# Values and three query units from rows that are not yet normed, and three exponentials some units later

## What is computed

```python
def rmsnorm(x, g):
    return x * rsqrt(mean(x * x, axis=-1) + EPS) * g

h = rmsnorm(x, g_mix)
q, k, v, f_logit, gb, gc_in, xc, g_attn, g_conv = split(h @ w_in)
attn = forgetting_attention(q, k, v, f_logit + b_f)          # 8 heads of 64
conv = gb * causal_depthwise_conv(gc_in * xc, conv_w)
x = x + (gated sum of the two branches) @ w_out
h = rmsnorm(x, g_ffn)
q = h @ w_q                                                  # 8 heads x 2 halves of 128
s1, s2 = q_half1 @ k1.T, q_half2 @ k2.T                      # scores against 128 keys each
v1, i1 = top_k(s1, 16); v2, i2 = top_k(s2, 16)
top_s, top_j = top_k(v1[:, None] + v2[None, :], 16)          # best 16 of 256 pairs
gates = softmax(top_s)
x = x + sum over the chosen 16384-expert ids of gates * gelu(h @ u[id]) * v[id]
...                                                          # a gated embedding and a last norm follow
```

## Time and profile before

| | |
|---|---|
| median of 3 runs | 1810.73 us (1810.68 to 1811.7) |
| the profiled execution, its own time | 1813.05 us |
| its span in the trace | 1810.3 us |
| TensorE busy | 1774.5 us, 98% of the span |
| VectorE, GpSimd, ScalarE busy | 1082.2, 916.2, 671.6 us |
| mean granted clock of TensorE | 0.996 of full speed |

### The profile page before, as it was taken

One profiled execution on the slowest core, in us unless ns is written; L12 is line 12 of the kernel. 1 busy time (PEld: TensorE's weight loads), 2 busy tenths in 40 slices (PEclk: granted clock), 3 DMA queues, 4 the chain that ended last, 5 costly groups with the idle time before them and its releaser, 6 DMA issues.

```text
span 1810.3 us, 22222 instructions
## 1 busy us (share of the span) xinstructions
PE 1774.5 (98%) x7972; PEld 1454.8 (80%) x7972; DVE 1082.2 (60%) x1929; ACT 671.6 (37%) x1031; POOL 916.2 (51%) x742
## 2 busy tenths in 40 slices
PE   6999999989999999999999999999999999999998
PEld 5777788878878788888888888888888888888886
DVE  6355521436799988862222221235888888888874
ACT  5434332333332222322222222244444444444464
POOL 6323244334336787776666666405566666664200
PEclk9999999989999999999999999999999999999999
DMA  5212122317775444444444444467999999999821
GB/s 193 88 59 71 59 93 93 116 59 312 269 242 176 148 144 145 147 146 146 146 146 144 148 146 134 144 214 249 371 374 367 373 361 382 381 364 379 318 82 47
DMA packets 155565, 360.99 MB, mean 199 GB/s; under 512 B 32064, under 2 KB 73024, under 8 KB 155328
## 3 DMA queue, kind: packets, MB, share of 16 engines
q1 hardware_dynamic: 100976, 257.47, 41.4%
q0 software_dynamic: 34816, 67.41, 10.4%
q10 hardware_dynamic: 19664, 34.70, 5.3%
HBM read 298.44 MB, written 61.01 MB: 199 GB/s over the span
## 4 chain that ended last, share of the span: by engine, by line
PE 92%; DVE 6%; ACT 1%; DMA 1%; issue 1%; ACTq 0%; DVEq 0%
PE pair L748 33%; PE pair L556 18%; PE pair L558 18%; PE pair L557 18%; PE pair L652 1%; PE pair L672 1%; PE pair L726 1%; DVE topj L1383 1%; DVE wl L1357 1%; DVE top L1381 1%; PE pair L642 0%; DVE earlier L1454 0%; DVE cand L1452 0%; DVE cand L1449 0%; PE pair L757 0%
## 5 line engine op out<-in xcount | busy, mean ns | idle before, releaser
L510 POOL DMA_INDIRECT gates<-gate_val,gate_at x384 | 415.1, 1081 | 203.8 <-issue 102.5
L1357 DVE TENSOR_TENSOR wl<-raw,wh 128x1024 fp32r<-128x1024 f32 x254 | 309.5, 1220 | 345.2 <-ACT wh L896 344.8
L896 ACT ACTIVATE wh<-raw 128x1024 fp32r<-128x1024 f32 x339 | 356.7, 1054 | 135.9 <-PE pair L558 123.2
L748 PE MATMUL pair<-hh,wh 128*128 128x512 f32 x1024 | 399.0, 390 | 3.6 <-ACT gout L1069 2.9
L748 PE MATMUL pair<-hl,wh 128*128 128x512 f32 x1024 | 398.6, 389 | 0.0
L748 PE MATMUL pair<-hh,wl 128*128 128x512 f32 x1024 | 398.5, 389 | 0.0
L493 POOL TENSOR_TENSOR wl<-raw,wh 128x1024 fp32r<-128x1024 f32 x85 | 207.2, 2443 | 332.7 <-ACT wh L896 332.7
L556 PE MATMUL pair<-wh,act_h 128*128 128x512 f32 x768 | 299.1, 389 | 0.0
L558 PE MATMUL pair<-wh,act_l 128*128 128x512 f32 x768 | 298.9, 389 | 0.0
L557 PE MATMUL pair<-wl,act_h 128*128 128x512 f32 x768 | 298.9, 389 | 0.0
L1069 ACT ACTIVATE gout<-pair 128x512 f32<-128x512 f32 x128 | 76.4, 597 | 471.9 <-PE pair L748 471.9
(11 more groups left out here) (234 smaller groups left out, 1907.1 us busy)
## 6 DMA issues: line engine op xcount, KB each, us to landing
raw<-stream SPq DMA_DIRECT2D x338, 512.0 KB, 3.6
score_dram<-gout ACTq DMA_DIRECT2D x128, 256.0 KB, 2.0
gates<-zeros SPq DMA_DIRECT2D x48, 512.0 KB, 6.0
score_in<-score_dram SPq DMA_DIRECT2D x128, 192.0 KB, 6.4
gate<-gates SPq DMA_DIRECT2D x128, 192.0 KB, 6.8
gates<-gate_val,gate_at POOLq DMA_INDIRECT x384
x<-xT SPq DMA_DIRECT2D x4, 512.0 KB, 5.2
picked<-score_dram,score_at POOLq DMA_INDIRECT x128, 5.7
```

The lines of the kernel that those rows point to most:

```text
L510: nc.gpsimd.indirect_dma_start(gate_list, bass.IndirectOffsetOnAxis(ap=gate_at[:, r, k:k + 1], axis=0), gate_val[:, r, k:k + 1], None).the ...
L748: last = nc.tensor.matmul(psum[u % 2][:], w(weights, U_DENSE + u, c), halves[:, c, :], start=c == 0 and which == 0, stop=c == DC - 1 and w ...
L896: nc.scalar.activation(wh[:, n % SL, :], raw[:, n % RAW, :], ACT.Copy).then_inc(hi_done, 1)
L1357: nc.vector.tensor_tensor(wl[:, n % SL, :], raw[:, n % RAW, :], wh[:, n % SL, :].bitcast(F32), ALU.subtract).then_inc(low_own, 1)
```

## The change

Values. The high and low parts of the V stage are taken from gain * x instead of the normed h (`plain_high`, `plain_low`), and the four copies out of PSUM carry `factor` as their scale. So V no longer waits for the norm. Each unit's 24 matmuls now go in three groups of eight (high, low activations, low weights); the norm's sums stand behind the first group of the second unit, and its rows behind that unit. The normed `hh` and `hl` are written into the same buffers afterwards, each pair of chunks once its V unit is done; the f logits read them. SyncE loads x and weight units in turns: x0, unit 0, x1, unit 1, x2, x3, unit 2.

Queries. The first three query units read `xh` and `xl`, made from gain * x chunk by chunk during the output units; `factor` is the scale of four copies of each unit's scores. The sums stand inside the first query unit, the rows behind it. Units 0 and 1 are no longer interleaved. The normed chunks are made beside these three units and are needed by the fourth.

Both norms keep their squares and products in PSUM (banks 4 and 5) instead of SBUF, and the table of Sqrt is loaded ahead. The exponentials of the second to fourth routing tile stand three dense units later; the first stays.

```diff
+PLAIN_PQ = 3
...
-EXP_AT = (3, 16, 32, 48)
+EXP_AT = (3, 19, 35, 51)
...
-        sq1 = gout[:, 0:2, :]
-        hf1 = gout[:, 2:4, :]
...
+        xh = sb("xh", [P, DC, T], F32R, plain)
+        xl = sb("xl", [P, DC, T], F32R, plain)
...
+                for i in {0: (0,), 1: (1,), 2: (2, 3)}.get(n, ()):
+                    load_x(i)
...
+            def values(j, part, weights, first, last_part):
+
+                for c in (2 * j, 2 * j + 1):
+                    if part is hl:
+                        pe.wait_ge(xl_ready, c + 1)
+                    elif first:
+                        pe.wait_ge(xh_ready, c + 1)
+                    for tt in range(TT):
+                        last = nc.tensor.matmul(psum[tt][:], part[:, c, tt * P:(tt + 1) * P],
+                                                weights[:, U_V + j, (c % 2) * CW:(c % 2 + 1) * CW],
+                                                start=first and c == 0, stop=last_part and c == DC - 1)
+                return last
...
-            norm_sums(0)
+            for j in range(4):
+                pe.wait_ge(hi_done, U_V + j + 1)
+                values(j, hh, wh, True, False)
+                if j == 1:
+                    norm_sums(0)
+                values(j, hl, wh, False, False)
+                wait_low(pe, U_V + j)
+                values(j, hh, wl, False, True).then_inc(unit_used, 1)
+                if j == 1:
+                    norm_rows(0)
             pe.wait_ge(wf_split, 1)
-            for j in range(4):
-                wait_low(pe, U_V + j)
-                for c in (2 * j, 2 * j + 1):
-                    pe.wait_ge(h_ready, c + 1)
-                    for tt in range(TT):
-                        cols = slice(tt * P, (tt + 1) * P)
-                        wc = slice((c % 2) * CW, (c % 2 + 1) * CW)
-                        last = three(psum[tt][:], hh[:, c, cols], hl[:, c, cols], wh[:, U_V + j, wc], wl[:, U_V + j, wc],
...
-                last = three(psum[4][0:HEADS, :], wf_h[:, c, :], wf_l[:, c, :], hh[:, c, :], hl[:, c, :], c == 0, c == DC - 1)
+                pe.wait_ge(h_ready, c + 1)
+                last = three(psum[6][0:HEADS, :], wf_h[:, c, :], wf_l[:, c, :], hh[:, c, :], hl[:, c, :], c == 0, c == DC - 1)
...
-            norm_sums(1)
...
-            pe.wait_ge(wo_out, DC)
-            project_pair(U_PQ, 0, h_ready, DC)
-            score(0)
-            for n in range(2, N_PQ):
-                pe.wait_ge(pq_out, n - 1)
-                project(U_PQ + n, n % 2)
-                score(n - 1)
+            pe.wait_ge(wo_out, DC - 2)
+            for n in range(N_PQ):
+                if n < PLAIN_PQ:
+                    if n >= 2:
+                        pe.wait_ge(pq_out, n - 1)
+                    wait_low(pe, U_PQ + n)
+                    plain_query(n, 0, 5)
+                    if n == 0:
+                        norm_sums(1)
+                    plain_query(n, 5, DC)
+                    if n == 0:
+                        norm_rows(1)
+                else:
+                    pe.wait_ge(pq_out, n - 1)
+                    if n == PLAIN_PQ:
+                        pe.wait_ge(h_ready, 2 * DC)
+                    project(U_PQ + n, n % 2)
+                if n >= 1:
+                    score(n - 1)
...
-            def square(k, sqb, c):
+            def square(k, c):
                 if c >= 2:
                     act.wait_ge(sq_used, DC * k + c - 1)
-                nc.scalar.activation(sqb[:, c % 2, :], x[:, c, :], ACT.Square).then_inc(sq_ready, 1)
+                nc.scalar.activation(psum[4 + c % 2], x[:, c, :], ACT.Square).then_inc(sq_ready, 1)
...
+            def normed_high(k, c):
+
+                act.wait_ge(hf_ready, DC * k + c + 1)
+                nc.scalar.activation(hh[:, c, :], psum[4 + c % 2], ACT.Copy).then_inc(hh_ready, 1)
+
+            def plain_high(k, high_part, c):
+
+                nc.scalar.activation(high_part[:, c, :], x[:, c, :], ACT.Copy, scale=gain[:, k, c:c + 1]).then_inc(xh_ready, 1)
...
+            act.wait_ge(consts, 6)
+            nc.scalar.activation(spare[:, 0:1], eps[:], ACT.Sqrt)
+            act.wait_ge(gain_in, 16)
+            for i in range(2):
+                act.wait_ge(x_in[i], 16)
+                plain_high(0, hh, 2 * i)
+                plain_high(0, hh, 2 * i + 1)
+                if i == 0:
+                    high(0)
+                square(0, 2 * i)
+                square(0, 2 * i + 1)
+            high(1)
+            for i in range(2, 4):
+                act.wait_ge(x_in[i], 16)
+                square(0, 2 * i)
+                square(0, 2 * i + 1)
+            for c in range(4, DC):
+                plain_high(0, hh, c)
+            high(2)
+            root(0)
+            high(3)
             for c in range(DC):
-                act.wait_ge(x_in[c // 2], 16)
-                square(0, sq, c)
-            high(0)
-            norm(0, hf, highs=((0, 1), (2, 2), (4, 3), (6, 4)))
-            for n in range(5, SL):
-                high(n)
+                if c == 6:
+                    act.wait_ge(unit_used, U_V + 4)
+                    for tt in range(TT):
+                        last = nc.scalar.activation(v_sb[:, tt, :], psum[tt][:], ACT.Copy, scale=factor[:, tt:tt + 1])
+                    last.then_inc(v_out, 1)
+                elif c % 2 == 0:
+                    act.wait_ge(unit_used, U_V + c // 2 + 1)
+                normed_high(0, c)
+                if c < 4:
+                    high(4 + c)
             for n in range(3):
                 next_high(U_V + n)
...
                 act.wait_ge(wo_out, c + 1)
-                square(1, sq1, c)
+                square(1, c)
+                plain_high(1, xh, c)
                 if c < DC - 1:
                     next_high(U_OUT + c)
-            norm(1, hf1)
-            next_high(U_OUT + DC - 1)
-
+            root(1)
...
+                if n < PLAIN_PQ:
+                    for tt in range(TT):
+                        last = nc.scalar.activation(scores[:, n % 2, tt, :], psum[2 + n % 2][:, tt * NK:(tt + 1) * NK], ACT.Copy,
+                                                    scale=factor[:, tt:tt + 1])
+                    last.then_inc(sc_out, 1)
+                    return
...
+            query_out(0)
+            for c in range(DC):
+                normed_high(1, c)
+                if c == 3:
+                    query_out(1)
+                elif c == 5:
+                    next_high(U_OUT + DC - 1)
+            next_high(U_PQ)
+            score_out(0)
+            next_high(U_PQ + 1)
+            for n in range(2, N_PQ):
+                query_out(n)
                 next_high(U_PQ + n)
-                if n >= 1:
-                    score_out(n - 1)
+                score_out(n - 1)
...
-            def add_square(k, sqb, c):
+            def add_square(k, c):
                 dve.wait_ge(sq_ready, DC * k + c + 1)
                 if c == 0:
-                    nc.vector.tensor_copy(rstd[:], sqb[:, 0, :]).then_inc(sq_used, 1)
+                    nc.vector.tensor_copy(rstd[:], psum[4]).then_inc(sq_used, 1)
                 else:
                     dve.wait_ge(sq_used, DC * k + c)
-                    nc.vector.tensor_tensor(rstd[:], rstd[:], sqb[:, c % 2, :], ALU.add).then_inc(sq_used, 1)
-
-            def norm(k, hfb):
+                    nc.vector.tensor_tensor(rstd[:], psum[4 + c % 2], rstd[:], ALU.add).then_inc(sq_used, 1)
...
-                        nc.vector.scalar_tensor_tensor(out=hfb[:, c % 2, :], in0=x[:, c, :], scalar=gain[:, k, c:c + 1],
+                        nc.vector.scalar_tensor_tensor(out=psum[4 + c % 2], in0=x[:, c, :], scalar=gain[:, k, c:c + 1],
...
-                        nc.vector.tensor_tensor(hl[:, c - 1, :], hfb[:, (c - 1) % 2, :], hh[:, c - 1, :].bitcast(F32),
+                        nc.vector.tensor_tensor(hl[:, c - 1, :], psum[4 + (c - 1) % 2], hh[:, c - 1, :].bitcast(F32),
...
+            def plain_low(k, high_part, low_part, c):
+
+                dve.wait_ge(xh_ready, DC * k + c + 1)
+                nc.vector.scalar_tensor_tensor(out=low_part[:, c, :], in0=x[:, c, :], scalar=gain[:, k, c:c + 1],
+                                               in1=high_part[:, c, :].bitcast(F32), op0=ALU.mult,
+                                               op1=ALU.subtract).then_inc(xl_ready, 1)
+
+            for i in range(2):
+                plain_low(0, hh, hl, 2 * i)
+                plain_low(0, hh, hl, 2 * i + 1)
+                add_square(0, 2 * i)
+                add_square(0, 2 * i + 1)
+            for c in range(4, DC):
+                add_square(0, c)
+            for c in range(4, DC):
+                plain_low(0, hh, hl, c)
+            dve.wait_ge(const_in, 48)
+            link(nc.vector.tensor_copy(wf_h[:], wf[:]))
+            nc.vector.tensor_tensor(wf_l[:], wf[:], wf_h[:].bitcast(F32), ALU.subtract).then_inc(wf_split, 1)
+            norm(0)
...
                 if dc >= 1:
-                    add_square(1, sq1, dc - 1)
```

(7 more changed lines are left out.)

63 lines of the change are left out of this document (27 added, 36 removed).

## The result

| | before | after |
|---|---|---|
| median | 1811.56 us (1810.68 to 1814.82, 6 runs) | 1796.89 us (1793.76 to 1798.73, 6 runs) |
| profiled execution, its own time | 1813.05 us | 1798.73 us |
| span in the trace | 1810.3 us | 1797.0 us |
| mean granted clock | 0.996 | 0.997 |

The ratio is 0.9915 with a 95% interval of 0.9902 to 0.9928: the change makes the kernel 0.85% faster. The forecast was 1794.3 us in a range of 1787.0 to 1800.5; the time lies in it, 2.6 us above the point.

What follows compares the result with a forecast made beforehand. TensorE was taken as the bound, with 92% of what ended last and busy for 98% of the span. The gains 8.0 + 6.1 + 2.3 = 16.4, subtracted from 1810.73, gave 1794.3 us, range 1787.0 to 1800.5.

Steps and rivals of the forecast that it cites:

- Start: Values stage: V starts at 7.0 us, first mixing unit at 41.2 instead of 49.20, 8.0 won, bounds 4.8 to 11.8.
- The lower level: First matmuls from 7.0 us: TensorE runs at the lower of its two speed levels, costing 2.0 us.
- The wait ahead of the rows: First norm: TensorE waits 2.7 us, bounds 0 to 3.5, for VectorE's diagonals, three held until GpSimd's second low part ends.
- The 0.5 for a lower level behind the wait: Behind the wait for the first norm's diagonals, TensorE may fall to its lower speed again; 0.5 us added.
- rival (c): Normed chunks still suffer from GpSimd although they read PSUM; f waits, some 6 us back, total 1800; chance 0.04.
- Rival (d): Clock stays at its lower level through V; 1815.8 us if all 120 matmuls are slow; chance 0.02.
- Queries: Three plain query units at the second norm: 9.8 won, less 2.8 wait and 0.9 lower level, 6.1; bounds 2.9 to 9.8.
- The term for the lower level, 0.9: Behind the wait at the third query unit's scores, TensorE's lower speed costs 0.9 us, taken between 0 and 2.6.
- Exponentials: Dense stage, later exponentials: TensorE's pause of 2.17 us ahead of 609.86 and some refill go, 2.3 us won.
- Nobody waits: Dense stage: the exponential moves to about 613, 4 to 5 us behind the routing, and no engine waits for it.
- Rival (e): Dense stage: the exponential at the second tile still blocks, +2.3 us, total 1796.6; chance 0.03.
- part 3: The later exponentials in the dense stage, forecast to win 2.3 us.

Runs made afterwards that it cites:

- spaced: Changed kernel with GpSimd's first 160 scatters paced at 3 per dense unit instead of 3.25, those behind four units later; 1794.30 us, ratio 0.9902.
- diag_free: Changed kernel with the first norm's root and diagonals ahead of unit 2's high part, and VectorE's split of f's weights behind them; 1795.06 us, ratio 0.9903.
- copies_first: Changed kernel with each query copy from the third on moved ahead of the high part that stood before it; 1793.88 us, ratio 0.9903.
- after_again: The changed kernel run once more, unchanged; 1796.88 us.
- exp_only: Kernel before with only the second to fourth tiles' exponentials moved, to dense units 19, 35 and 51; 1812.07 us, ratio 1.000.
- exp_second: Changed kernel with exponentials at dense units 3, 19, 32 and 48, only the second tile's later; 1796.91 us, ratio 0.9924.
- copy_first: Changed kernel with only the third query unit's copy moved ahead of the high part before it; 1797.04 us, ratio 0.9910.
- exp_third: Changed kernel with exponentials at dense units 3, 16, 35 and 48, only the third tile's later; 1797.63 us, ratio 0.9924.
- exp_spaced: Kernel before with late exponentials (19, 35, 51) and GpSimd's first 160 scatters paced at 3 per dense unit; 1809.18 us, ratio 0.9979.
- best: Changed kernel with the edits of copies_first and diag_free, the pace of spaced, and the first exponential at dense unit 5; 1788.64 us, ratio 0.9870.

## Why the prediction was right where it was, and where it was not

**Start, forecast 8.0, measured 8.95.** V was to start at 7.0 and did at 7.15. The lower level was to cost 2.0; 3.55 us for eight matmuls and 2.04 for the next eight, against 1.82 each, make 1.95. The wait ahead of the rows was foreseen with its cause and mis-sized: 1.68 instead of 2.7. The working let the rows begin when all four diagonals were made; each row piece waits only for its own, so they began at 22.79, with the first, while the fourth ended at 23.3. It also had the wrong instruction slip in between GpSimd's two low parts: it was the split of f's weights, and all four diagonals waited for the second. The two terms are not independent either. The rows begin at 22.7 to 22.8 in all nine kernels that have this wait, whether the slow pitch ended early and TensorE waited 1.96 us or late and it waited 0.84: what the slow pitch costs ahead of the rows, the wait gives back. The 0.5 for a lower level behind the wait did not come in after; in spaced it came and cost 1.6. That VectorE's instructions with SBUF operands are held up by GpSimd's low parts and those with a PSUM operand are not is shown by diag_free and by the normed chunks, 0.69 to 0.76 us each, also beside the four low parts that GpSimd makes from 26.46 on: rival (c) is out. The Trainium skill's page "SBUF — State Buffer", section "Who interferes with whom", has this rule, and the rows agree with it (2.32 against 0.22 us). Rival (d) is out as well: in after the slow pitch ended before 12 us.

**Queries, forecast 6.1, measured 5.3 in after and 7.4 in its repeat.** The chain of events was right: third query copy behind a high part, that one behind a transfer. Moved by the 8.95 us of the start, TensorE was released at 413.41 + 8.95 = 422.4 where the forecast had 422.5; it arrived 0.7 later than forecast, nearly all of it by a longer wait for the gates' rows in the first attention stage (1.20 us against 0.54 to 0.74 in most other kernels), so the wait was 1.92 instead of 2.8. The term for the lower level, 0.9, is a mean of two cases: of seven kernels with this wait four ran slowly behind it and lost 1.6, three lost nothing. copies_first shows the wait gone; its dense stage starts 1.35 us earlier than in after_again, and the 0.95 us lost to the later high part would have come on top.

**Exponentials, forecast +2.3, measured -1.5.** This is the step that failed, at the words "Nobody waits". Alone it would have been a slip of 3.8 us. That the pause ahead of 609.86 goes, that the one at the first tile stays (0.69) and that VectorE needs the exponentials late enough all came true. The working followed the three engines named in the rows and left out the fourth: GpSimd's scatters, paced by the same signal of TensorE, had been level with it at the end of unit 32, in part by that pause, and now were 2.9 to 4.1 us behind. The signal of dense unit 32 was 5.8 to 7.0 us late in all seven kernels with a late second exponential and the old pace (exp_only, after, after_again, exp_second, copy_first, diag_free, copies_first). It was on time in the four with the early one (the 0.5 us that one expectation names was the exponential ahead of the copy, and its 1.2 us belong to unit 31 of exp_third), and on time in the three with late exponentials and the new pace (spaced, exp_spaced, best).

**Rival (e)** gave 1796.6, which is close to the 1796.89 measured, but it is not what happened: the late exponentials don't block. The time agrees because another loss of about the same size came. The gain of 0.6 behind the dense stage was not in the sum.

**Together.** The parts missed by +0.95, -0.8, -3.8 and +0.6, which is 3.1 us of the 16.4 by the spans and 1.7 by the medians (14.7 won). Parts 1 and 2 were right in mechanism, both waits included. That the total lies in the range in spite of part 3 is the width of a range that added the worst bounds, and not a sign that part 3 was understood.

## What to carry to other kernels

A pause of the busiest engine may be what lets a slower follower catch up; before taking it out, look at every engine that is paced by the same signal, also the one that nobody waits for in the trace. An engine's list should hold nothing that the critical engine needs behind an instruction that waits for a transfer; moving only the first such instruction moved the wait to the next, and moving all of them put one high part, 0.95 us, ahead of the last copy that the next stage needed. Small VectorE instructions on the critical path belong ahead of GpSimd's long ones, not beside them.
